# Dilated attention at the end of a two-block network: values product in quarters, scaled output one pair later

## What is computed

```python
q = rms_norm(heads(a_q), q_norm_g)
k = rms_norm(heads(a_k), k_norm_g)
v = heads(a_v)
outs, lses = zip(*[dilated_window_attention(q, k, v, rel_bias, w, d) for w, d in DILATED_PATTERNS])
weights = jax.nn.softmax(jnp.stack(lses), axis=0)
o = jnp.sum(weights[..., None] * jnp.stack(outs).astype(jnp.float32), axis=0)
```

## Time and profile before

| | us |
|---|---|
| median of 3 runs | 2536.44 |
| lowest and highest | 2535.78 to 2536.64 |
| profiled execution, whole time | 2539.14 |
| its span, first to last instruction | 2537.3 |
| TensorE busy | 2349.0 (93%) |
| VectorE, ScalarE, GpSimd busy | 1001.8, 616.4, 114.4 |
| attention steps 0 to 15, in the span | from about 1444 to 1524 |
| part 5 of the projection ends on TensorE | 1537.6 |
| experts' products, first to last | 1602 to 2534 |

### The profile page before, as it was taken

One profiled execution on the slowest core, in us unless ns is written; L12 is line 12 of the kernel. 1 busy time (PEld: TensorE's weight loads), 2 busy tenths in 40 slices (PEclk: granted clock), 3 DMA queues, 4 the chain that ended last, 5 costly groups with the idle time before them and its releaser, 6 DMA issues.

```text
span 2537.3 us, 24160 instructions
## 1 busy us (share of the span) xinstructions
PE 2349.0 (93%) x10181; PEld 1407.2 (55%) x10181; DVE 1001.8 (39%) x1610; ACT 616.4 (24%) x1001; POOL 114.4 (5%) x120
## 2 busy tenths in 40 slices
PE   5999989899999999999999988989898998989888
PEld 2445544588888788888777647524242333323232
DVE  4555463466663566665666353211111110101001
ACT  2112153333223333233456464100000000000000
POOL 2000000000000000000221322000000000000000
PEclk8999988999999899999999998999999999999999
DMA  9312230355553155551221205699999999999997
GB/s 360 108 67 83 100 133 1 116 191 187 179 196 124 50 166 199 183 199 35 88 68 34 79 30 232 258 430 431 431 430 431 430 430 431 431 430 428 431 431 306
DMA packets 122386, 594.09 MB, mean 234 GB/s; under 512 B 10674, under 2 KB 12224, under 8 KB 96678
## 3 DMA queue, kind: packets, MB, share of 16 engines
q1 hardware_dynamic: 118850, 583.18, 57.9%
q0 software_dynamic: 3120, 9.24, 1.1%
q10 hardware_dynamic: 308, 0.13, 0.0%
HBM read 590.39 MB, written 2.14 MB: 234 GB/s over the span
## 4 chain that ended last, share of the span: by engine, by line
PE 77%; DMA 14%; DVE 6%; ACT 2%; issue 1%; POOL 0%; DVEq 0%; ACTq 0%; POOLq 0%
PE PS L1231 15%; PE PS L912 9%; PE PS L913 9%; PE PS L914 9%; PE PS L965 6%; PE PS L709 6%; PE PS L149 5%; PE PS L1248 3%; PE PS L1258 2%; PE PS L871 2%; DMA RING<-in_w_gate_dram 2%; DMA RB_a<-in_w_down_dram 2%; DMA RB_a<-in_w_gate_dram 2%; DMA RING<-in_w_down_dram 2%; PE PS L793 2%; DMA RING<-in_w_up_dram 2%
## 5 line engine op out<-in xcount | busy, mean ns | idle before, releaser
L1231 PE MATMUL PS<-RING,HID_e 128*64 128x512 f32 x592 | 206.4, 611 | 11.1 <-DMA RING<-in_w_gate_dram 5.9
L1231 PE MATMUL PS<-RB_a,HID_e 128*64 128x512 f32 x576 | 200.2, 606 | 9.0 <-DMA RB_a<-in_w_up_dram 5.4
L2578 DVE TENSOR_TENSOR TMP<-TMP,PS 128x512 f32<-128x512 f32 x32 | 19.8, 682 | 359.7 <-PE PS L1231 359.7
L1231 PE MATMUL PS<-HID_e 128*64 128x512 f32 x304 | 136.0, 595 | 5.0 <-DMA HID_e<-in_w_gate_dram 2.6
L1231 PE MATMUL PS<-XT,HID_e 128*64 128x512 f32 x288 | 130.4, 602 | 7.7 <-DMA XT<-in_w_up_dram 5.1
L1231 PE MATMUL PS<-AT_g,HID_e 128*64 128x512 f32 x288 | 132.0, 607 | 3.6 <-DMA AT_g<-in_w_gate_dram 2.6
L1787 ACT ACTIVATE HID_e<-PS,cmat 128x128 f32<-128x128 f32 x32 | 12.1, 456 | 486.7 <-PE PS L149 486.7
L1231 PEld LDWEIGHTS PS<-RING,HID_e 128*64 128x64 f32 x592 | 63.7, 140 | 101.2 <-issue 82.4
L2586 DVE TENSOR_TENSOR HID_e<-PS,HID_e 128x512 f32<-128x512 f32 x16 | 10.3, 686 | 270.9 <-PE PS L1248 270.9
L1248 PE MATMUL PS<-RING,HID_e 128*64 128x512 f32 x304 | 106.2, 619 | 11.4 <-DMA RING<-in_w_down_dram 11.4
L1248 PE MATMUL PS<-RB_a,HID_e 128*64 128x512 f32 x288 | 105.3, 621 | 10.6 <-DMA RB_a<-in_w_down_dram 10.6
(11 more groups left out here) (465 smaller groups left out, 4670.1 us busy)
## 6 DMA issues: line engine op xcount, KB each, us to landing
RING<-in_w_up_dram SPq DMA_DIRECT2D x19, 2048.0 KB, 18.7
RING<-in_w_down_dram SPq DMA_DIRECT2D x19, 2048.0 KB, 22.0
RING<-in_w_gate_dram SPq DMA_DIRECT2D x18, 2048.0 KB, 22.6
RB_a<-in_w_gate_dram SPq DMA_DIRECT2D x18, 2048.0 KB, 22.0
RB_a<-in_w_up_dram SPq DMA_DIRECT2D x18, 2048.0 KB, 17.9
RB_a<-in_w_down_dram SPq DMA_DIRECT2D x18, 2048.0 KB, 22.0
RING<-in_mlp_w_dram SPq DMA_DIRECT2D x32, 1024.0 KB, 5.5
RB_a<-in_mlp_w_dram SPq DMA_DIRECT2D x32, 1024.0 KB, 5.2
```

Source lines behind the costliest of these rows:

```text
L1231: last = pe.matmul(b[64 * d:64 * d + 64, :], xv_[:, k, 64 * d:64 * d + 64], wv, start=k == 0, stop=k == 7)
L2578: dve.tensor_tensor(q, q, banks.of("up", n, fg), ALU.mult).then_inc(*V_moe.up("act", n, fg))
```

## The change

- The values product and the spread of pair hp are cut into quarters st = 0 to 3 and placed behind the turning of the four steps of the next pair; those of pair 3 stand together behind block 1 of part 5.
- `PTs` gets a fourth buffer, in the place of `kf`; the first time it is written, ScalarE waits until GpSimd has done block 3 of the projection's operand.
- Every bank gets a fixed seat: logits in 0 to 3 (by the parity of the step), the turned tiles in 4 and 5, values in 6, spread in 7. So the turning of step s waits for ScalarE's copies of step s - 1, and the values of a pair for the `out` of the pair before.
- ScalarE's copy of the spread bank and VectorE's `out` of pair hp move from step 4 (hp + 1) to step 4 (hp + 2), and those of pair 2 behind the last step; `high(4)` and `high(5)` move to steps 9 and 13.
- Of part 5, one block instead of three is done among the steps (in step 15), one behind the last turning, and six behind the values of pair 3. GpSimd takes block 4 of the weights ahead of block 6 of the operand.

```diff
--- before.py
+++ after.py
@@ -344,7 +344,7 @@
         av = CAT3[:, 0:4, :]
         aq = H(4096, hid=HID3)
         ak = H(8192, hid=HID3)
-        PTs = Turns([H(o, hid=HID3) for o in (10240, 12288, 0)])
+        PTs = Turns([H(o, hid=HID3) for o in (10240, 12288, 0, 6144)])
         Gb = [HID3[:, o:o + 896] for o in (2048, 2944, 14336, 15232)]
         half_sum = blk64[:, 0:128:64]
         qk_gain, eps64 = ST[:, 364:365], ST[:, 365:366]
@@ -557,9 +557,10 @@
                 pool_bias(pool, w, h)
                 if h % 2:
                     pool_out2(pool, w, 2 + h // 2)
+            pool_part(pool, w, 5, 4)
             pool_out2(pool, w, 6)
-            for k in (4, 5, 6):
-                pool_part(pool, w, 5, k)
+            pool_part(pool, w, 5, 5)
+            pool_part(pool, w, 5, 6)
             pool_out2(pool, w, 7)
             pool_part(pool, w, 5, 7)
             for k in range(8):
@@ -1092,7 +1093,7 @@
             hp, i = s // 4, s % 4
             w.wait_ge(*S_dil.at("aq", "out", hp))
             w.wait_ge(*S_dil.at("ak", "out", 3))
-            bs = [banks.take(w, ("logits", s, c), (V_dil, "logit", s, c)) for c in range(2)]
+            bs = [banks.seat(w, 2 * (s % 2) + c, ("logits", s, c), (V_dil, "logit", s, c)) for c in range(2)]
             for c, b in enumerate(bs):
                 p = slice(64 * c, 64 * c + 64)
                 pe.matmul(b, aq[p, hp, i * 128:(i + 1) * 128], ak[p, hp, :], start=True, stop=True).then_inc(
@@ -1100,29 +1101,33 @@
 
         def pe_dil_turn(pe, w, s):
             for c in range(2):
-                b = banks.take(w, ("dturn", s, c), (S_dil, "turn", s, c))
+                b = banks.seat(w, 4 + c, ("dturn", s, c), (S_dil, "turn", s, c))
                 w.wait_ge(*S_dil.at("exp", s, c))
                 lg = lg_tmp.of("logit", s, c)
                 transposes(pe, b, [lg[:, st * 128:(st + 1) * 128] for st in range(4)]).then_inc(*T_dil.up("turn", s, c))
 
-        def pe_dil_values(pe, w, hp):
-            b = banks.take(w, ("dpv", hp), (V_dil, "out", hp))
+        def pe_dil_values(pe, w, hp, st):
+
+            if st:
+                b, b2 = banks.of("dpv", hp), banks.of("dspread", hp)
+            else:
+                b = banks.seat(w, 6, ("dpv", hp), (V_dil, "out", hp))
+                b2 = banks.seat(w, 7, ("dspread", hp), (S_dil, "spread", hp))
             w.wait_ge(*S_dil.at("turn", 4 * hp + 3, 1))
             w.wait_ge(*S_ml.at("av", 3))
-            for st in range(4):
-                for c in range(2):
-                    h = 2 * hp + c
-                    last = pe.matmul(b[64 * c:64 * c + 64, :], av[:, st, h * 64:(h + 1) * 64], PTs.of(h)[:, st, :],
-                                     start=st == 0, stop=st == 3)
-            last.then_inc(*T_dil.up("pv", hp))
-            b = banks.take(w, ("dspread", hp), (S_dil, "spread", hp))
+            for c in range(2):
+                h = 2 * hp + c
+                last = pe.matmul(b[64 * c:64 * c + 64, :], av[:, st, h * 64:(h + 1) * 64], PTs.of(h)[:, st, :],
+                                 start=st == 0, stop=st == 3)
+            if st == 3:
+                last.then_inc(*T_dil.up("pv", hp))
             w.wait_ge(*V_dil.at("recip", 4 * hp + 3))
-            for i in range(4):
-                for c in range(2):
-                    last = pe.matmul(b[64 * c:64 * c + 64, i * 128:(i + 1) * 128],
-                                     soft(4 * hp + i, 3)[:, c:c + 1].to_broadcast([128, 64]), ident[:, :],
-                                     start=True, stop=True)
-            last.then_inc(*T_dil.up("spread", hp))
+            for c in range(2):
+                last = pe.matmul(b2[64 * c:64 * c + 64, st * 128:(st + 1) * 128],
+                                 soft(4 * hp + st, 3)[:, c:c + 1].to_broadcast([128, 64]), ident[:, :],
+                                 start=True, stop=True)
+            if st == 3:
+                last.then_inc(*T_dil.up("spread", hp))
 
         def pe_dil_key_turn(pe, w, i):
             b = banks.seat(w, 4 + i, ("kturn", i), (S_dil, "ak", "out", i))
@@ -1143,28 +1148,25 @@
             pe_parts(pe, w, 4, bs, (6, 7), AH3, AL3, fed6)
             for j in range(3):
                 pe_dil_rows(pe, w, j)
-            banks.i = 0
             pe_dil_logits(pe, w, 0)
             pe_dil_rows(pe, w, 3)
-            banks.i = 2
             pe_dil_logits(pe, w, 1)
             for s in range(16):
                 if s < 14:
                     pe_dil_logits(pe, w, s + 2)
+                if s == 15:
+                    bs = pe_open(pe, w, 5, lambda j: ((V_out, "out2", j, 0),), (0, 1, 2, 3))
+                    pe_parts(pe, w, 5, bs, range(1), AL3, AH3, out2_fed)
                 pe_dil_turn(pe, w, s)
-                if s % 4 == 0 and s:
-                    pe_dil_values(pe, w, s // 4 - 1)
-                if s == 13:
-                    bs = pe_open(pe, w, 5, lambda j: ((V_out, "out2", j, 0),))
-                if s >= 13:
-                    pe_parts(pe, w, 5, bs, (s - 13,), AL3, AH3, out2_fed)
-            banks.i -= 4
-            pe_dil_values(pe, w, 3)
-            pe_parts(pe, w, 5, bs, range(3, 8), AL3, AH3, out2_fed)
-            banks.i -= 2
-            bs = pe_open(pe, w, 6, lambda j: ((V_out, "out2", 4 + j, 0),))
+                if s > 3:
+                    pe_dil_values(pe, w, s // 4 - 1, s % 4)
+            pe_parts(pe, w, 5, bs, range(1, 2), AL3, AH3, out2_fed)
+            for st in range(4):
+                pe_dil_values(pe, w, 3, st)
+            pe_parts(pe, w, 5, bs, range(2, 8), AL3, AH3, out2_fed)
+            bs = pe_open(pe, w, 6, lambda j: ((V_out, "out2", 4 + j, 0),), (4, 5, 6, 7))
             pe_parts(pe, w, 6, bs, range(4), AL3, AH3, out2_fed)
-            rbs = [banks.take(w, ("router", i), (V_moe, "logits", i)) for i in range(4)]
+            rbs = [banks.seat(w, i, ("router", i), (V_moe, "logits", i)) for i in range(4)]
             pe_router(pe, w, rbs, range(4))
             pe_parts(pe, w, 6, bs, range(4, 8), AL3, AH3, out2_fed)
             pe_router(pe, w, rbs, range(4, 8))
@@ -1749,6 +1751,8 @@
                     if i == 0:
                         PTs.take(w, (h,), (T_dil, "pv", hp))
                         w.wait_ge(*V_ml.at("ho", 3, 2))
+                        if h == 3:
+                            w.wait_ge(*G_out.at("lo", 3))
                     w.wait_ge(*T_dil.at("turn", s, c))
                     act.activation(PTs.of(h)[:, :, i * 128:(i + 1) * 128],
                                    banks.of("dturn", s, c).rearrange("p (k n) -> p k n", n=128), ACT.Copy, bias=0.0,
@@ -1757,12 +1761,14 @@
                     act_part(act, w, 5, 1 + s)
                 if s < 4:
                     high(s)
-                if i == 0 and s:
-                    spread(hp - 1)
-                elif i == 2 and s > 4:
-                    high(3 + hp)
-                if s >= 14:
-                    act_part(act, w, 5, s - 10)
+                if i == 0 and hp > 1:
+                    spread(hp - 2)
+                elif i == 1 and hp > 1:
+                    high(2 + hp)
+            spread(2)
+            act_part(act, w, 5, 4)
+            high(6)
+            act_part(act, w, 5, 5)
             spread(3)
             act_part(act, w, 5, 6)
             high(7)
@@ -2474,8 +2480,9 @@
                     logits(s + 1)
                 w.wait_ge(*S_dil.at("exp", s, 1))
                 dve.reciprocal(soft(s, 3), soft(s, 2)).then_inc(*V_dil.up("recip", s))
-                if s % 4 == 0 and s:
-                    out(s // 4 - 1)
+                if s % 4 == 0 and s > 4:
+                    out(s // 4 - 2)
+            out(2)
             out(3)
 
         def dve_out2(dve, w):
```

## The result

The changed kernel takes 2543.8 us (median of 9 runs, 2541.4 to 2546.1) where the kernel before takes 2536.4 (9 runs on the same chip, 2533.0 to 2538.9). The ratio is 1.0029, with a 95% interval of 1.0020 to 1.0038: **7.4 us slower (5.1 to 9.6)**. The profiled execution took 2544.49 us with a span of 2542.7, against 2539.14 and 2537.3.

What follows compares the result with a forecast made beforehand. The end was taken to follow TensorE's end of part 5, with VectorE pacing the steps. Gains nearly lost to the bias wait, then a longer TensorE tail, put part 5 4.2 us later: 2536.44 + 4.2 = 2540.6 us, range 2534.5 to 2544.5.

Steps and rivals of the forecast that it cites:

- (a): First pair boundary, VectorE: no wait for the spread bank, step 6's logits start at 1465.6, a gain of 5.7 us.
- (b): Behind the first boundary: the bias of head 4 lands at 1473.0 and VectorE's logits of step 8 start then.
- (c): Second boundary: spread copy stands behind ScalarE's exponentials and copies; VectorE idles 3.0 us instead of 4.85 before `out`.
- (d): GpSimd's queue: head 6's bias transfer, behind `pool_out2(4)`, lands at 1494.4; VectorE waits 5.6 us for it at step 12.
- (e): Third boundary: step 14's logits start at 1504.1 against 1506.64, VectorE 2.5 us ahead of before.
- (f): TensorE's tail: put-off work, with 0.7 us for seams and 1.1 for the clock, ends part 5 4.2 us later.
- Rival A: Bias is in time at step 12; part 5 ends 1.4 to 2.5 us sooner, 2534 to 2535 us; chance 0.14.
- Rival B: TensorE stays busy through the boundaries; 6 us or more of 12.1 idle vanish, 2530 or below; chance 0.04.
- Rival C: TensorE becomes the bound, 3.2 us per step against VectorE's 3.03, plus seams and low clock: 2543.6 us; chance 0.17.

Runs made afterwards that it cites:

- e1: The changed kernel with GpSimd's two differences put behind the last bias transfers: 2539.6 us.
- e4: The kernel before with only `high(4)` moved on ScalarE from step 6 to step 9: 2543.7 us.
- e7: The kernel before with GpSimd's differences of the two scaled outputs put behind the last bias transfers: 2536.0 us.
- e9: e3 with GpSimd's block of four differences spread out, each put where its ScalarE step is done: 2529.96 us.
- e2: The changed kernel with ScalarE copying the spread bank ahead of the next exponentials at a pair's first step: 2534.9 us.
- e5: The changed kernel with TensorE repeating logits in its idle time at two boundaries, logits of steps 11 and 15 moved ahead of the values quarter: 2539.2 us.
- e3: The changed kernel with both edits, bias transfers first (e1) and spread copy early (e2): 2530.0 us.
- e6: e3 with a pair's four values quarters all computed at the first step of the pair two later: 2533.8 us.
- e8: e3 with VectorE's negation written in a form with two inputs: median 2526.6 us.
- e10: e3 unchanged, run once more as e9's neighbour on the same chip: 2531.4 us, ratio 0.9976 to the kernel before.

## Why the prediction was right, and where it was off

The forecast was 2540.6, the time is 2543.8, near the upper end of the range; the mechanism named as the one that decides is the one that the trace and e1, e4 and e7 show. Set on the clock of the changed kernel's trace (1.67 us less than the prediction's, which used the trace of before), point by point:

- **(a)** Step 6's logits were to start at 1465.6 - 1.67 = 1463.9 and did at 1464.59. TensorE's turning begins at 1463.21 and was in time (VectorE follows it by 0.69 elsewhere, which gives 1463.90). The 0.65 is the long negation of step 5, which the prediction did not have. The wait for the spread bank near there is gone as said.
- **(b)** Step 8's logits: 1471.3 forecast, 1471.29 measured, but for another reason, so the number is luck. The trace names TensorE's turning as what ended the 0.60 wait; it began at 1470.60, 0.69 earlier. The bias of head 4, issued at 1466.98, must have landed at much the same time. e9 parts the two: there the bias was issued 5.12 us ahead of step 8's logits instead of 4.31, and they still start 0.70 behind the beginning of the turning.
- **(c)** 3.0 us of wait ahead of each `out` forecast, 3.04 twice measured; e2 shows that the place of the spread copy is their whole cause. Ahead of the second boundary a step goes at 3.31 us (1471.29 to 1474.60), not 3.03, which puts `out` 0.3 us later than forecast.
- **(d)** The bias wait: 5.6 forecast, 3.87 measured. The moment was right (step 12 at 1494.4 - 1.67 = 1492.7 forecast, 1493.12 measured, `high(4)` at 1487.11 plus 6.01 instead of 6.33), but VectorE came to it at 1489.25, 2.1 us later than forecast, mostly since it had waited 1.65 for TensorE at step 11. The low clock at the second boundary was missing from the sum, and it was free, as the wait swallowed it. So the wait came out 1.7 us shorter than forecast without step 12 coming any sooner: VectorE had lost that time before it. By the Trainium skill's figure the transfer would have landed 1.3 us sooner than the earlier trace rows has it; from issue to VectorE's start it took 4.08 us here, 4.14 in e2, 4.15 in e4 and 4.31 in e5, so the row was the better price.
- **(e)** Logits of step 14 at 1504.1 - 1.67 = 1502.4 forecast, 1502.90 measured.
- **(f)** This is the term that was mis-sized. From the first quarter of pair 2 to the end of part 5 the sum has 37.5 us and the trace 1541.60 - 1503.04 = 38.56. The clock was put at 1.1. Measured, the quarter took 2.33, the logits 2.01 and the turning 1.84, against 1.23, 1.06 and 1.02 at full clock: 2.9. The wait of 0.6 for the copies, which was to swallow part, never came, because the slow TensorE was late itself. A quarter is 1.23 and not 1.11, as each has its own seams, but that 0.5 and 0.3 in the blocks are what the 0.7 for seams had allowed for. So 1.1 is missing here (1.8 of clock less the wait of 0.6), and 0.4 came in from (a) to (e): 4.2 + 1.5 is the 5.7 that the trace has.

The last 1.7 us between 5.69 and the median's 7.4 lie within the interval. In the two profiled executions, from the first exponentials to the end, the difference is 7.07 us, 5.71 of it up to the eighth transfer and 1.36 behind it; that last stretch scatters from 926.5 to 929.2 us over the twelve traces, so no cause can be given for the 1.36.

**Rival A** (bias in time) is out: the wait is there, and even with it taken away (e1) the kernel is not faster. **Rival B** (the idle time goes) was right about the kernel's potential and wrong about this change: its 2530 takes both e1's and e2's edit (e3). **Rival C** (TensorE the bound) was given 0.17 and 2543.6, and a good part of it came true beside (d): steps of 3.31 on TensorE, VectorE waiting 0.6, 0.19, 1.65 and 2.52 for its turning, and a low clock in the tail. What it priced as 0.2 on each quarter is 0.12 (1.23 for 1.11). The forecast treated C as something instead of (d); they add up, and the sum should have carried the low clock at its full price, read off the same rows 4 and 10 that it quoted.

## What to carry to other kernels

When a step is moved back on one engine, go through the in-order queue of every engine that waits for it and ask what stands behind that wait: here one small difference on GpSimd held two unrelated transfers, which cost 4.6 us of the attention (e1). A piece that is released early but issued late (the spread copy behind exponentials and copies) is found by the gap between release and start, and is put right by moving one call. And an idle gap on TensorE should be priced twice, as the gap and as the low clock of the work behind it, if that work is what the end waits for; where another wait follows, as at e5's second boundary, the low clock costs nothing.

## What the runs showed of the hardware

A VectorE instruction on two columns took 1.20 to 1.22 us instead of 0.17 in eight traces (the changed kernel, e1, e2, e3, e5, e6, e8, e10), always beside a GpSimd difference and always ending with it. Three further cases in the same stage fit as well: in e5 the negation at 1508.16 takes 1.09 and ends with a difference that began at 1507.97; in the changed kernel the negation at 1511.42 takes 0.41 and ends 0.03 behind a difference that began at 1510.54 with 1.26, and in e1 one of 0.25 at 1486.58 behind one from 1485.54. Writing it with two inputs changed nothing (e8); moving GpSimd's work away removed it (e9). In the kernel before the same block of four stood there too, but the negation (1464.86, 0.17) fell on the seam between two of them (1463.72 + 1.24 = 1464.96). The Trainium skill (SBUF — State Buffer, section on who interferes with whom) says that VectorE and GpSimd share one pair of ports to the scratch memory, that it is held for a whole instruction, and that both a single-input `tensor_scalar` and an instruction with two inputs there can be the one shut out; the traces agree. VectorE's instructions with one operand in the matmul's output memory (the logits, 0.72 to 0.75) were never stretched beside the same differences, and neither were the row maxima, which read and write the scratch memory (0.69 each time).

Work that nobody needs made a kernel faster: with the gaps at the two boundaries filled, TensorE held 2.4 GHz from 1480 to 1486 and from 1501 to 1510 (e5), where the changed kernel had been granted 0.80 and 0.63, and 0.71, 0.50 and 0.65, and the attention became 2.35 us shorter.

TensorE's clock also fell without a gap: in part 6 of the projection, behind 32 small products of the router that took 3.64 us, the kernel before was granted 0.72 and 0.50 from 1551.78 to 1555.78 while busy all the time. In e3, e8 and e10 it kept 1.00 at the same place, and the fifth write into `XT` came 1.6 us sooner.
